# A mixture-of-experts encoder layer on one core: the last stage with a buffer for every tile, early residual loads, and its gate on GpSimd

## What is computed

```
h   = rms_norm(x1, g_ffn) * (1 + sc2) + sh2
out = w0 * y[expert 0 of the token] + w1 * y[expert 1 of the token]     # hier_moe(h)
x2  = x1 + gt2 * out                                                    # gt2: one row of 1024
return rms_norm(x2, g_final)
```

## Time and profile before

| | us |
|---|---|
| median of 3 runs | 3035.41 (3032.02 to 3035.68) |
| the profiled execution, its own time | 3033.13 |
| its span | 3031.0 |
| PE busy | 2752.4 (91%) |
| DVE busy | 1731.7 (57%) |
| ACT busy | 1500.7 (50%) |
| POOL busy | 817.5 (27%) |
| last matmul ended | 2929.9 |
| experts done, `yp` loads begin | 2937.1 |

### The profile page before, as it was taken

One profiled execution on the slowest core, in us unless ns is written; L12 is line 12 of the kernel. 1 busy time (PEld: TensorE's weight loads), 2 busy tenths in 40 slices (PEclk: granted clock), 3 DMA queues, 4 the chain that ended last, 5 costly groups with the idle time before them and its releaser, 6 DMA issues.

```text
span 3031.0 us, 50427 instructions
## 1 busy us (share of the span) xinstructions
PE 2752.4 (91%) x14228; PEld 2316.2 (76%) x14229; DVE 1731.7 (57%) x3141; ACT 1500.7 (50%) x2615; POOL 817.5 (27%) x617
## 2 busy tenths in 40 slices
PE   8899999999999997899999799939999999999950
PEld 2399999999888786688888678727788888888840
DVE  3555655556677675645441143457866735365868
ACT  2455666766545444344432132216766634365854
POOL 1244444545422211334444211101211111111210
PEclk9999999999999998899999899959999999999985
DMA  7500000000000001334343343328987846476988
GB/s 269 201 24 25 25 24 24 25 25 25 21 19 17 11 10 59 124 127 139 131 131 113 125 171 143 138 111 308 378 311 271 318 165 228 145 280 255 390 318 328
DMA packets 195890, 451.20 MB, mean 149 GB/s; under 512 B 39958, under 2 KB 91158, under 8 KB 193772
## 3 DMA queue, kind: packets, MB, share of 16 engines
q1 hardware_dynamic: 176812, 389.46, 36.2%
q0 software_dynamic: 14400, 52.44, 4.7%
q10 hardware_dynamic: 4608, 8.39, 0.7%
HBM read 380.01 MB, written 70.21 MB: 149 GB/s over the span
## 4 chain that ended last, share of the span: by engine, by line
PE 73%; DVE 8%; issue 8%; DMA 6%; ACT 3%; POOL 1%; SPq 1%; DVEq 0%; ACTq 0%; POOLq 0%
PE bank L1691 14%; PE bank L1906 14%; PE bank L1790 5%; PE bank L1834 4%; PE S_ps L1917 3%; PE E_ps L1917 3%; PE O_ps L1756 3%; DMA sb_w_in<-in_w_gate_up 3%; PE S_ps L1790 3%; PE S_ps L1737 3%; PE E_ps L1790 3%; PE S_ps L1739 3%; PE bank L1657 2%; PE E_ps L1723 2%; PE S_ps L1834 1%
## 5 line engine op out<-in xcount | busy, mean ns | idle before, releaser
L1906 PE MATMUL bank<-sb_gu,sb_x_hiT 128*128 (+1 forms) x1568 | 493.4, 396 | 11.4 <-DVE sb_x_loT L1552 8.5
L726 POOL TENSOR_TENSOR sb_h_lo<-sb_hT,sb_h_hi 128x1024 fp32r<-128x1024 f32 x128 | 337.2, 2635 | 610.4 <-ACT sb_h_hi L841 610.4
L1691 PE MATMUL bank<-sb_w_hi,sb_h_hi 128*128 (+1 forms) x1024 | 401.8, 392 | 15.5 <-issue 9.1
L1906 PEld LDWEIGHTS bank<-sb_gu,sb_x_hiT 128*128 128x128 f32 x1568 | 293.4, 189 | 73.4 <-issue 11.0
L1691 PE MATMUL bank<-sb_w_hi,sb_h_lo 128*128 (+1 forms) x1024 | 344.5, 336 | 0.0
L1691 PE MATMUL bank<-sb_w_lo,sb_h_hi 128*128 (+1 forms) x1024 | 343.7, 336 | 0.0
L1538 DVE TENSOR_TENSOR sb_gu<-sb_w_in,sb_gu 128x1024 f32 (+1 forms) x256 | 301.1, 1220 | 64.2 <-ACT sb_gu L1071 62.4
L1071 ACT ACTIVATE sb_gu<-sb_w_in 128x1024 f32 (+1 forms) x256 | 257.1, 1059 | 104.8 <-DMA sb_w_in<-in_w_gate_up 80.5
L1906 PE MATMUL bank<-sb_gu,sb_x_loT 128*128 (+1 forms) x784 | 308.3, 393 | 0.0
L765 POOL TENSOR_TENSOR sb_g_lo<-sb_g_raw,sb_g_hi 128x1408 fp32r<-128x1408 f32 x64 | 212.5, 3342 | 341.3 <-ACT sb_g_hi L946 341.3
L1691 PEld LDWEIGHTS bank<-sb_w_hi,sb_h_hi 128*128 128x128 f32 x1024 | 193.7, 189 | 31.2 <-issue 19.1
(11 more groups left out here) (346 smaller groups left out, 6113.8 us busy)
## 6 DMA issues: line engine op xcount, KB each, us to landing
sb_w_in<-in_w_gate_up SPq DMA_DIRECT2D x256, 512.0 KB, 6.2
sb_w_in<-in_w_expert_down SPq DMA_DIRECT2D x128, 512.0 KB, 5.2
sb_g_raw<-in_w_gb SPq DMA_DIRECT2D x64, 704.0 KB, 4.1
sb_wada<-in_w_ada SPq DMA_DIRECT2D x24, 1024.0 KB, 8.0
sb_yp<-y_d SPq DMA_DIRECT2D x16, 1024.0 KB, 6.8
sb_w_raw<-in_w_qkv SPq DMA_DIRECT2D x128, 96.0 KB, 2.0
sb_x_round<-in_x SPq DMA_DIRECT2D x4, 2048.0 KB, 12.6
mT_d<-sb_mg ACTq DMA_DIRECT2D x32, 256.0 KB, 2.1
```

Of the source, the lines that this page charges most:

```text
L726: nc.gpsimd.tensor_tensor(h_lo[c][:], tile_src(g, T), h_hi[c][:].bitcast(F32), ALU.subtract).then_inc(sem("h_lo_ready"), 1)
L1691: last = nc.tensor.matmul(bank[c][:, 0:PASS_COLS].rearrange("p (a m) -> p a m", a=1), x[c][:, k, :], w[:, ds(row + k, 1), :], start=(k == ...
L1906: last = nc.tensor.matmul(PS[j][:].rearrange("p (a n) -> p a n", a=1), x[:, k, :], gu[:, ds(gu_row(e, part, k), 1), j * DE:(j + 1) * DE], ...
```

## The change

The last stage gets a `yp` buffer for each of the 16 tiles: six in front (where other expert buffers were), eight in the first half of `gu`, two in the ring. `acc` is gone: every step works in place in `yp[t][:, 0, :]`. All 16 residual tiles `xl` lie in the second half of `gu` and are loaded by four DMAs of 2 MB as soon as ACT says, at the start of expert 31 (`half_free`, when the last gate/up product of expert 30 is done), that this half is empty. All 16 `yp` loads are issued at once when the experts are done; the stores follow. ACT weighs tile t, then squares tile t-3. DVE has `mix` (the old L1604), `add_residual` two tiles behind, `means` and `finish` once per two tiles; between `mix` and `add_residual`, POOL multiplies the row by `gt2b`. All loops of the stage are written out, and the semaphores of earlier stages are used again for the new buffers (`Y_IN`, `X1_IN`).

```diff
--- before.py
+++ after.py
@@ -42,12 +42,13 @@
 ROUNDS = SEQ // P // ROUND
 NORM_FROM = 4
 assert 2 * (N_MOD * D // CHUNK - NORM_FROM) == TT
-LAG = ROUND + 1
+PAIRS = TT // 2
+W_LOADS = 8 * 16 // 2
 RING = 6
 PIECES = KD + KE
 assert PIECES == 2 * RING
 
...
 
 MOD_CHUNKS = N_MOD * D // CHUNK
@@ -304,26 +305,31 @@
     dn_hi = m8("dn_hi", [P, KE, D], F32R)
     dn_lo = m8("dn_lo", [P, KE, D], F32R)
 
+    gu_at = m8.at
     gu = m8("gu", [P, 4 * KD, 2 * DE], F32R)
     assert m8.at - 2 * KD * 2 * DE * 4 >= m6.at
 
     ring_at = m8.at
     w_in = [m8(f"w_in{s}", [P, 2 * DE]) for s in range(RING)]
     assert m8.at <= nc.sbuf_usable_end, (m8.at, nc.sbuf_usable_end)
-    m9 = Plan(tables.at)
-    yp = [m9(f"yp{r}", [P, 2, D]) for r in range(ROUND)]
-    acc = m9("acc", [P, 2 * ROUND, D])
-    sq3 = m9("sq3", [P, D])
-    ssq3 = m9("ssq3", [P, ROUND])
-    ms3 = m9("ms3", [P, ROUND])
-    rms3 = m9("rms3", [P, ROUND])
-    rstd3 = m9("rstd3", [P, ROUND])
-
-    assert m9.at <= ring_at
+
+    assert E % 2 == 0 and 2 * KD == TT and 2 * DE == D
+    xl = Plan(gu_at + TT * D * 4)("xl", [P, TT, D])
     early = Plan(ring_at)
     gt2b = early("gt2b", [P, D])
     gfb = early("gfb", [P, D])
-    xl = [early(f"xl{r}", [P, D]) for r in range(ROUND)]
+    m9 = Plan(tables.at)
+    front = (6, 8, 2)
+    yp = [m9(f"yp{t}", [P, 2, D]) for t in range(front[0])]
+    sq3 = m9("sq3", [P, D])
+    ssq3 = m9("ssq3", [P, TT])
+    ms3 = m9("ms3", [P, TT])
+    rms3 = m9("rms3", [P, TT])
+    rstd3 = m9("rstd3", [P, TT])
+    assert m9.at <= gu_at
+    for place, n in ((Plan(gu_at), front[1]), (early, front[2])):
+        yp += [place(f"yp{len(yp) + i}", [P, 2, D]) for i in range(n)]
+    assert len(yp) == TT and early.at <= nc.sbuf_usable_end
 
     bank = [ctx.enter_context(nc.psum_tensor(f"bank{i}", [P, 512], F32)) for i in range(3)]
     S_ps = ctx.enter_context(nc.psum_tensor("S_ps", [P, 2, 512], F32))
@@ -386,6 +392,18 @@
 
         first = 2 if j % RING >= 2 * RING - KD else 1
         return 16 * (first + 2 * e + j // RING + 1)
+
+
+
+    ring_loads = lambda slot: ring_count(E - 2, slot + RING) // 16 + (slot >= 2)
+    Y_IN = [(f"ring_in{s}", 16 * (ring_loads(s) + 1)) for s in range(RING)]
+    Y_IN += [(f"x_in{c}", 16 * (ROUNDS // 2 + TT // 2 + 1)) for c in range(2)]
+    Y_IN += [(f"od_in{c}", 16 * (TT + 1)) for c in range(2)]
+    Y_IN += [(f"mT_out{c}", 16 * (CHUNKS * KD // 2 + 2)) for c in range(2)]
+    Y_IN += [(f"w_in{c}", 16 * (W_LOADS + 1)) for c in range(2)]
+    Y_IN += [(f"o_out{c}1", 16 * (TILES_PER_GROUP // 2 + 1)) for c in range(2)]
+    X1_IN = [(f"m_in{c}", 16 * (TT // 2 + 1)) for c in range(2)] + [(f"g_in{c}", 16 * (CHUNKS * KD + 1)) for c in range(2)]
+    assert len(Y_IN) == TT
 
     def group_of(T):
         return min(max(T, 0) // TILES_PER_GROUP, 3)
@@ -419,9 +437,6 @@
                 straight(T)
         for T in range(STEPS, STEPS + 3):
             straight(T)
-
-    def acc_row(t):
-        return acc[:, ds(t % (2 * ROUND), 1), :].rearrange("p a n -> p (a n)")
 
     JOBS = ([(0, "b", k) for k in range(4)], [(u, "a", k) for k in range(2) for u in range(2)], [(1, "b", k) for k in range(4)],
@@ -646,49 +661,23 @@
             dn_piece(E - 1, k, (KD + k) % RING)
 
+        sp.wait_ge(sem("half_free"), 1)
+        x1v = x1_d.rearrange("(t p) n -> p t n", p=P)
+        for r in range(4):
+            sp.dma_start(xl[:, 4 * r:4 * r + 4, :], x1v[:, 4 * r:4 * r + 4]).then_inc(sem(X1_IN[r][0]), 16)
         sp.wait_ge(sem("dn_lo_ready"), KE * E)
         for t, row in ((gt2b, rows_d[5:6, :]), (gfb, A["g_final"].rearrange("(a n) -> a n", a=1))):
             sp.dma_start(t[:], row.broadcast_to([P, D])).then_inc(sem("rows_in"), 16)
         yv = y_d[0:2 * SEQ, :].rearrange("(t p two) n -> p t two n", p=P, two=2)
-        x1v = x1_d.rearrange("(t p) n -> p t n", p=P)
         ov = out.rearrange("a (t p) n -> p (a t) n", p=P)
 
-        def x1_in(t, r):
-            sp.dma_start(xl[r][:], x1v[:, ds(t, 1)].rearrange("p a n -> p (a n)")).then_inc(sem(f"slot_in{r}"), 16)
-
-        def outputs_in(t, r):
-            sp.dma_start(yp[r][:], yv[:, ds(t, 1)].rearrange("p a two n -> p (a two) n")).then_inc(sem(f"slot_in{r}"), 16)
-
-        def last_out(t, r):
+        sp.wait_ge(sem("experts_done"), 1)
+        for t in range(TT):
+            sp.dma_start(yp[t][:], yv[:, t]).then_inc(sem(Y_IN[t][0]), 16)
+        for t in range(TT):
             sp.wait_ge(sem("out_ready"), t + 1)
-            sp.dma_start(ov[:, ds(t, 1), :].rearrange("p a n -> p (a n)"), acc_row(t)).then_inc(sem(f"out_stored{r}"), 16)
-
-        for r in range(ROUND):
-            sp.sem_inc(sem(f"out_stored{r}"), 16)
-            x1_in(r, r)
-        sp.wait_ge(sem("experts_done"), 1)
-        for r in range(ROUND):
-            outputs_in(r, r)
-
-        def last_round(q, more):
-            for r in range(ROUND):
-                t = ROUND * q + r
-                if more:
-                    sp.wait_ge(sem("acc_ready"), t + 1)
-                    outputs_in(t + ROUND, r)
-                    x1_in(t + ROUND, r)
-                if not isinstance(t, int) or t >= LAG:
-                    last_out(t - LAG, (r - LAG) % ROUND)
-
-        last_round(0, True)
-        last_round(1, True)
-        with sp.Fori(2, TT // ROUND - 1) as q:
-            last_round(q, True)
-        last_round(TT // ROUND - 1, False)
-        for t in range(TT - LAG, TT):
-            last_out(t, t % ROUND)
-        for r in range(ROUND):
-            sp.wait_ge(sem(f"out_stored{r}"), 16 * (TT // ROUND + 1))
+            sp.dma_start(ov[:, t, :], yp[t][:, 0, :]).then_inc(sem("out_stored"), 16)
+        sp.wait_ge(sem("out_stored"), 16 * TT)
 
     @block.gpsimd
@@ -830,6 +819,11 @@
         pool.wait_ge(sem("y_out"), 16 * total)
         pool.wait_ge(sem("xg_in"), 16 * (total + 2))
         pool.sem_inc(sem("experts_done"), 1)
+
+        pool.wait_ge(sem("rows_in"), 112)
+        for t in range(TT):
+            pool.wait_ge(sem("mixed"), t + 1)
+            nc.gpsimd.tensor_tensor(yp[t][:, 0, :], yp[t][:, 0, :], gt2b[:], ALU.mult).then_inc(sem("gated_rows"), 1)
 
     @block.scalar
@@ -1130,10 +1124,12 @@
                 with act.If(e < E - 1):
                     next_expert_high(g, e, EARLY)
                     block_head(g)
-                    next_expert_high(g, e, LATE)
+                    next_expert_high(g, e, LATER)
                     block_tail(g)
                     down_high(g, e)
                 with act.Else():
+                    act.wait_ge(sem("gu_done"), g)
+                    act.sem_inc(sem("half_free"), 1)
                     block_head(g)
                     block_tail(g)
                     down_high(g, e, 16)
@@ -1143,38 +1139,26 @@
         rows_out(total - 1)
 
-        def weigh(q, r):
-            t = ROUND * q + r
-            act.wait_ge(sem(f"slot_in{r}"), 16 * (MOD_LOADS + OUT_LOADS) + 32 * (q + 1))
-            wait(act, sem(f"out_stored{r}"), 16 * q)
-            act.sem_inc(sem("last_waits"), 1)
-            w0 = pair_w[:, ds(t, 1), 0:1].rearrange("p a b -> p (a b)")
-            nc.scalar.activation(acc_row(t), yp[r][:, 0, :], ACT.Copy, scale=w0).then_inc(sem("first_weighed"), 1)
-
-        def roots(q):
-            act.wait_ge(sem("meansq"), ROUNDS + TT + q + 1)
-            nc.scalar.activation(rms3[:], ms3[:], ACT.Sqrt).then_inc(sem("rms"), 1)
-
-        def last_round(q, more):
-            for r in range(ROUND):
-                if r < ROUND - 1:
-                    weigh(q, r + 1)
-                elif more:
-                    weigh(q + 1, 0)
-                if r == 0 and not (isinstance(q, int) and q == 0):
-                    roots(q - 1)
-                t = ROUND * q + r
-                wait(act, sem("sumsq"), 2 * TT + t)
-                act.wait_ge(sem("acc_ready"), t + 1)
-                act.sem_inc(sem("last_waits"), 1)
-                nc.scalar.activation(sq3[:], acc_row(t), ACT.Square, accum_out=ssq3[:, r:r + 1]).then_inc(sem("sumsq"), 1)
-
-        weigh(0, 0)
-        last_round(0, True)
-        with act.Fori(1, TT // ROUND - 1) as q:
-            last_round(q, True)
-        last_round(TT // ROUND - 1, False)
-        roots(TT // ROUND - 1)
+        def weigh(t):
+            act.wait_ge(sem(Y_IN[t][0]), Y_IN[t][1])
+            nc.scalar.activation(yp[t][:, 0, :], yp[t][:, 0, :], ACT.Copy, scale=pair_w[:, t, 0:1]).then_inc(sem("first_weighed"), 1)
+
+        def squares_of(t):
+            act.wait_ge(sem("acc_ready"), t + 1)
+            wait(act, sem("sumsq"), 2 * TT + t)
+            nc.scalar.activation(sq3[:], yp[t][:, 0, :], ACT.Square, accum_out=ssq3[:, t:t + 1]).then_inc(sem("sumsq"), 1)
+
+        def roots(r):
+            act.wait_ge(sem("meansq"), ROUNDS + TT + r + 1)
+            nc.scalar.activation(rms3[:, 2 * r:2 * r + 2], ms3[:, 2 * r:2 * r + 2], ACT.Sqrt).then_inc(sem("rms"), 1)
+
+        for t in range(TT + 4):
+            if t < TT:
+                weigh(t)
```

(87 more changed lines are left out.)

2 lines of the change are left out of this document (1 added, 1 removed).

## The result

The changed kernel is slower, by more than forecast: median 3055.85 us (3051.22 to 3057.36, 4 runs) against 3035.55 us (4 runs of the kernel before beside it), ratio 1.0065 with a 95% interval of 1.0048 to 1.0082. The forecast was 3046.5 and its range ended at 3055.

A forecast was written before the change was run, and what follows sets the result against it. Last stage bound by DVE (busy 79.0 of 93.9 us) and nearly by DMA; afterwards DVE 56.6 + POOL turns 36.0 + end 3.1 = 95.7 against 84.4 us, +11.3, so 3046.5 us, range 3038 to 3055.

The forecast's parts named there:

- The direction, and that POOL's time comes on top of DVE's: Last stage: slower, since POOL's multiplication and DVE's instructions with two SBUF inputs take turns; 36.0 us added to DVE's 56.6.
- The price of a turn: Last stage: each POOL multiplication holds DVE for 2.40 - 0.15 = 2.25 us per tile, 36.0 us in all.
- the sum: DVE's last-stage stretch: 56.6 own work + 36.0 POOL turns + 3.1 end = 95.7 us, against 84.4 before.
- The estimate of 19.8 us: Slowdown if hand-overs followed the skill page's 115 ns after the winner's end, 8.5 us more than the measured hand-over gives.
- What is late next: Last stage: DVE's 1.6 us wait after every second tile's means, five times, hidden by POOL's instruction; 3.1 us at the end.
- I take no change: Last stage's start: early residual loads beside the last scatter leave it unchanged, bounds -1.8 and +3.2 us.
- The 20 us for 8.4 MB: Early residual loads: four of 2 MB from about 2910 at 420 GB/s, in at about 2931 to 2934.
- a first weighing later than 5 us: Sign of being wrong: ACT's first weighing that late after the experts are done, from 16 loads landing together.
- the scatter before: End of the experts: the second-to-last scatter may take 8.4 us, since the next eviction stands behind the last matmul.
- The chain means, root, weighing, mix: Last stage: DVE idle about 1.6 us, five times, waiting for ACT's next weighing; POOL's pending instruction runs in that gap.
- The one without exclusion: Rival: POOL and DVE do not lock in the last stage; DVE's stretch 73.9 us, median 3024.9; chance 0.08.
- The lock costs more: Rival: POOL's instruction takes 2.91 us, +7.3 (median 3054), or last scatter lands in 8.4 us, +3.2 (3049.9); chance 0.15.

The follow-up runs named there:

- e2: Changed kernel with the small means instruction writing to PSUM instead of SBUF; median 3046.99 us, ratio 1.0034 to the kernel before.
- e3: Changed kernel with the four residual loads issued after output tiles 1, 5, 9 and 13; median 3052.07 us, ratio 1.0052 to the kernel before.
- e6: Changed kernel with three residual loads early and the fourth after output tile 8; median 3050.15 us, ratio 1.0048 to the kernel before.
- e1: Changed kernel with the gate multiplication back on DVE, all else as changed; median 3038.76 us, ratio 1.001 to the kernel before.
- e5: Changed kernel with POOL's multiplication replaced by memsets that read nothing, gate left out; one run, 3032.11 us.
- e7: Changed kernel with means, weighed rows and a copy of the final gain in PSUM; median 3027.63 us, ratio 0.9971 to the kernel before.
- e9: Changed kernel with gate on DVE, means folded into ACT's square root, fourth residual load after output tile 8; median 3026.91 us, ratio 0.9975 to the kernel before.
- e10: Changed kernel with the means folded into ACT's square root, so no means instruction; median 3043.23 us, ratio 1.0029 to the kernel before.
- e8: Changed kernel with weighed rows and final gain in PSUM, means folded into ACT's square root, fourth residual load later, gate on POOL; median 3019.18 us, ratio 0.9948.

## Why the prediction was wrong

Two steps failed, the order of work behind `means` and the start. The profiled span grew by 18.5 us where +11.3 was forecast: 4.7 more in DVE's stretch and 5.8 in the start, less 3.1 and 0.2 for the experts' end and the stores. Two more us of the median's miss come from the profiled execution, which lay 4.6 us below its median and not 2.3. With the first fault undone the median is 3046.99 (e2), with the second undone in part 3052.07 and 3050.15 (e3, e6): it took both to leave the range, by 0.85 us.

- **The direction, and that POOL's time comes on top of DVE's: right.** The groups, e1, e5 and e7 show it from four sides: without POOL's multiplication, with POOL not reading, and for the two DVE lines that read PSUM, the long instructions are as quick as before.
- **The price of a turn, forecast 2.25 us: slightly too high.** A held instruction took 3.37 instead of 1.28 or 4.38 instead of 2.48, so 1.9 to 2.1 us. It began about 0.2 us before POOL's end (POOL's multiplication from 2954.30 to 2957.57, the `mix` beside it out at 2958.65 with 1.28 of its own), as in rows 7 and not after it. In e2, where the means are not held, the stretch is 92.7 us against the 95.7 of the sum. The estimate of 19.8 us in the prediction, by a later hand-over, came near the measured 18.5 by luck, since 5.8 of these are the start.
- **"What is late next": the first step that failed.** The forecast took `means` as 0.2 us and said that POOL's instruction runs in the gap behind it. But `means` itself waited for POOL, 2.30 us, and the gap came after POOL's turn rather than beside it. That is 100.4 - 92.7 = 7.7 us of stretch, measured by e2; the turn's lower price hides 3.0 of them. The rows had only shown DVE instructions with two SBUF inputs being held, and a small one-input instruction was not looked at. The Trainium skill (SBUF — State Buffer, "Who interferes with whom") lists `tensor_scalar` among those that can use both port pairs and so contend. The Trainium skill (VectorE: DVE Perf Modes, "Why PSUM operands drop a tier") rules such a mode out with an operand in PSUM. By both, e2 (0.15 us in PSUM) and e5 (0.87 us beside a memset) agree. That a 128x2 instruction uses that mode, no run shows other than by this waiting.
- **"I take no change" for the start, bounds -1.8 and +3.2: the second step that failed, outside the bounds.** It was +5.8 us. The 20 us for 8.4 MB left out the scatters, gathers, weights, `gt2b` and `gfb` on the same DMA engines: 397 GB/s over 27 us are 10.7 MB, and the engines were still full at 2937. The scatter alone, 7.5 us for 5.2, was within the bounds. The first output tile, in the queue behind the rest, was not priced at all: 8.1 us instead of 4.8. The prediction did name a first weighing later than 5 us as a sign of being wrong, but for another reason, loads that land together; they landed in turn. That the scatter before could take its 8.4 us held only just: at 7.8 us it ended with the last matmul, and in e9, at 8.2, it ended 0.5 us behind it.
- **The chain means, root, weighing, mix: right in size, wrong in place.** It was forecast at 1.6 us five times and measured at 1.3 of idle and 0.16 of means. Said to be covered, it is covered in e2 and e10 (92.7 and 91.2), but not where the means themselves are held, and not in e1, where it ate what the buffers gained.
- **The rivals.** The one without exclusion (3024.9) fell. Its sum for DVE alone, 73.9 us, agrees with e5 and e7 (73.7 and 74.1) in part by luck: e5 still contains held means (5.6 us for eight, against 1.3 in e1) and e7 held additions (24.3 us against 19.4), so for the case without any exclusion the sum is too long by some 4 us, an estimate from these two. "The lock costs more" had the size but not the cause. POOL's instructions did take 3.26 us, but with the wait for the turn in it: the first two took 2.35, and those that were issued 0.16 us behind a running addition took 0.9 more. (16 x 0.51 is 8.2 and not the 7.3 written there.) Of its other half, the longer scatter, 2.3 of 3.2 us came.

## What to carry to other kernels

Before moving work to POOL, list what DVE reads and writes meanwhile: here its instructions with two SBUF inputs, and a 128x2 `tensor_scalar` from SBUF to SBUF, took turns with a POOL instruction that reads SBUF, and with an operand in PSUM they did not. The first form of the change lost 20 us. With `mix` and `finish` reading PSUM, the means folded into ACT's square root and one residual load later, it won 16 (e8); 8 of these come without POOL (e9). Look at what hangs behind a held instruction, not only at its own length. And a load moved early is only free if all bytes of the stretch fit into it with time to spare: here a scatter on the path, and the first load behind it, paid 5.6 us for 8.4 MB in front.

## What the runs showed of the hardware that was not expected

- A `tensor_scalar` of 128x2 float32, SBUF to SBUF, took 2.30 us behind POOL's multiplication, 0.87 us behind a memset of POOL, and 0.15 us when it wrote to PSUM; a reciprocal of the same size passed in 0.16 us during POOL's turn.
- POOL's memset (0.95 us) held none of the 48 long DVE instructions; nearly each of its 16 multiplications held one DVE instruction.
- One operand of a 128x1024 `scalar_tensor_tensor` in PSUM cost DVE nothing (1275 to 1279 ns, against 1278 to 1283 unheld with all operands in SBUF).
- The last indirect scatter of 128 rows landed in 3.3 us where the DMA engines were busy for 0.37 of that time (e3), in 5.2 in the kernel before, and in 7.3 to 8.0 in eight of the nine kernels with early residual loads (5.9 in e8).

Left open: whether the residual addition of e8 can be freed too, by another order or by a third operand in PSUM; it was not tried.
